# A decoder trunk kernel: small matrix products of the RWKV-7 recurrence on four array quarters, weight splits in pieces, operands built at other points

## The reference, cut to what matters

```python
def rwkv7_time_mix(p, mu, ...):            # 8 heads of 64
    r, k, v, zw, za, zg = _split(p + (prev - p) * mu, ...)
    kk = (k * k_k).reshape(B, T, H, N)
    kk = kk / jnp.maximum(jnp.sqrt(jnp.sum(kk * kk, -1, keepdims=True)), 1e-12)
    ...
    def step(S, inp):
        r_t, w_t, k_t, v_t, a_t, b_t = inp          # a = -kk, b = kk * a
        sa = jnp.einsum('bhij,bhj->bhi', S, a_t)
        S = S * w_t[:, :, None, :] + sa[..., None] * b_t[:, :, None, :] + v_t[..., None] * k_t[:, :, None, :]
        y = jnp.einsum('bhij,bhj->bhi', S, r_t)
        return S, y
    _, y = lax.scan(step, S0, xs)
    y = (y - mean) * lax.rsqrt(var + RWKV_LN_EPS)   # then ln_w, ln_b, bonus, gate
```

## Time and profile before

| | us |
|---|---|
| median of 3 runs | 1079.82 |
| lowest, highest | 1078.2, 1080.12 |
| the profiled execution | 1081.36 |
| its span (first to last instruction) | 1079.6 |
| of it PE busy | 1045.2 |
| DVE, POOL, ACT busy | 527.5, 496.8, 355.8 |

### The profile page before, as it was taken

One profiled execution on the slowest core, in us unless ns is written; L12 is line 12 of the kernel. 1 busy time (PEld: TensorE's weight loads), 2 busy tenths in 40 slices (PEclk: granted clock), 3 DMA queues, 4 the chain that ended last, 5 costly groups with the idle time before them and its releaser, 6 DMA issues.

```text
span 1079.6 us, 18610 instructions
## 1 busy us (share of the span) xinstructions
PE 1045.2 (97%) x7560; PEld 836.0 (77%) x7560; DVE 527.5 (49%) x882; ACT 355.8 (33%) x688; POOL 496.8 (46%) x409
## 2 busy tenths in 40 slices
PE   7989999999999999999989999999999999999997
PEld 6777778887787677766777777888888888888886
DVE  4775687466555545554552664144454545430004
ACT  4133332221322225444550445352222222221221
POOL 3365453113121446655777447534444444444462
PEclk9999999999999999999999999999999999999999
DMA  9334533002223453212112545603333333333322
GB/s 253 95 98 138 115 88 80 3 4 59 61 61 100 120 142 118 59 32 79 40 39 79 175 118 167 213 27 91 97 97 97 97 97 97 116 98 98 98 79 78
DMA packets 148784, 102.67 MB, mean 95 GB/s; under 512 B 20917, under 2 KB 131775, under 8 KB 148712
## 3 DMA queue, kind: packets, MB, share of 16 engines
q1 hardware_dynamic: 145516, 97.67, 31.9%
q10 hardware_dynamic: 3164, 3.97, 1.5%
q0 software_dynamic: 32, 0.00, 0.0%
HBM read 93.99 MB, written 7.63 MB: 94 GB/s over the span
## 4 chain that ended last, share of the span: by engine, by line
PE 83%; DVE 9%; POOL 4%; issue 2%; ACT 1%; DMA 1%; SPq 0%; ACTq 0%; DVEq 0%; POOLq 0%
PE ps L1546 17%; PE ps L1548 15%; PE ps L1547 15%; PE ps L1685 4%; PE ps L2001 4%; PE ps L2000 4%; PE ps L1999 4%; PE ps L1592 4%; PE ps L1845 3%; PE ps L1897 2%; DVE XF L1074 1%; PE ps L1921 1%; PE ps L1922 1%; PE ps L1923 1%; POOL WLO L605 1%
## 5 line engine op out<-in xcount | busy, mean ns | idle before, releaser
L605 POOL TENSOR_TENSOR WLO<-WRAW,WHI 128x1024 fp32r<-128x1024 f32 (+1 forms) x131 | 293.9, 2244 | 283.6 <-ACT WHI L723 158.0
L1546 PE MATMUL ps<-HHI,WHI 128*128 128x512 f32 x776 | 316.9, 408 | 5.1 <-POOL WLO L640 2.3
L1548 PE MATMUL ps<-HHI,WLO 128*128 128x512 f32 x776 | 304.3, 392 | 0.0
L1547 PE MATMUL ps<-HLO,WHI 128*128 128x512 f32 x776 | 304.1, 392 | 0.0
L1546 PEld LDWEIGHTS ps<-HHI,WHI 128*128 128x128 f32 x776 | 146.6, 189 | 57.7 <-issue 22.0
L1548 PEld LDWEIGHTS ps<-HHI,WLO 128*128 128x128 f32 x776 | 146.5, 189 | 32.0
L1547 PEld LDWEIGHTS ps<-HLO,WHI 128*128 128x128 f32 x776 | 146.8, 189 | 29.3 <-issue 1.9
L609 POOL CAST WHI<-WRAW 128x256 fp32r<-128x256 f32 (+1 forms) x78 | 49.2, 631 | 179.8 <-PE ps L1548 179.8
L723 ACT ACTIVATE WHI<-WRAW 128x1024 fp32r<-128x1024 f32 (+1 forms) x69 | 62.5, 907 | 159.4 <-PE ps L1548 82.0
L1504 DVE TENSOR_TENSOR FT<-FT 128x512 f32<-128x512 f32 x22 | 51.6, 2348 | 89.0 <-ACT FT L977 89.0
L870 ACT ACTIVATE EB<-EB,STAT 128x257 f32<-128x257 f32 (+5 forms) x96 | 50.4, 527 | 55.7 <-DVE STAT L1388 54.6
(11 more groups left out here) (311 smaller groups left out, 1608.1 us busy)
## 6 DMA issues: line engine op xcount, KB each, us to landing
WRAW<-in_w_in SPq DMA_DIRECT2D x47, 512.0 KB, 4.3
WRAW<-in_w_gate SPq DMA_DIRECT2D x22, 512.0 KB, 3.9
WRAW<-in_w_up SPq DMA_DIRECT2D x22, 512.0 KB, 3.9
WRAW<-in_w_down SPq DMA_DIRECT2D x22, 512.0 KB, 3.9
spilled<-SQ SPq DMA_DIRECT2D x21, 256.0 KB, 2.5
WRAW<-in_w_in SPq DMA_DIRECT2D x16, 256.0 KB, 3.6
WRAW<-in_w_branch SPq DMA_DIRECT2D x32, 128.0 KB, 2.9
WRAW<-in_w_out SPq DMA_DIRECT2D x8, 512.0 KB, 4.0
```

The lines of the kernel that those rows point to most:

```text
L605: return pool.tensor_tensor(lo[:, 0:chunks, :], WRAW[:, n % NRAW, 0:chunks, :], hi[:, 0:chunks, :].bitcast(F32), ALU.subtract)
L1546: pe.matmul(dst, WHI[:, s, k, :], hi, start=start, stop=False)
L1547: pe.matmul(dst, WHI[:, s, k, :], lo, start=False, stop=False)
L1548: return pe.matmul(dst, WLO[:, s, k, :], hi, start=False, stop=stop)
```

## The change

1. **Quarters.** XS, UI and T1 live in the other half of the partitions. U is formed `across` (operands in one half, result in the other: quadrants (0,1) and (1,0) in turns). In levels 1 to 4 the XC and XS products of a chunk are issued head by head: two of XC across, two of XS along the diagonal, into different PSUM banks. T1 and the state's part of y are interleaved likewise. ACT now copies XC of both chunks, then XS of both.
2. **Level 0.** PE forms both AM'·I and I·AM (64 matmuls per pass instead of 32) behind one increment; DVE makes XC and XS each in one op of 512 columns from PSUM.
3. **DVE's order.** evacs(pt + 1) and (pt + 2) move from ahead of level 1 into level 4; evacs(pt + 12) moves behind AR of the next pass; `scaled_bk(cp + 1)` moves from the first chunk to the end of the pass.
4. **Pieces.** Splitting by two chunks begins at job 28 (PIECE0) instead of 49.
5. **Operands.** XF of the second compression is built one quarter at a time (after NSA tile 5 and after mixed 4, 5, 6); its low and high part, the broadcast of kk and the product with it each come one RWKV tile later.
6. **Norm.** gn_bonus(1) comes ahead of inverse_split(1) on DVE.

```diff
-POOL_HI = [1] + list(range(NS0 + 4, MERGE0))
+PIECE0 = NS0 + 4
+POOL_HI = [1] + list(range(PIECE0, MERGE0))
...
-            for n in range(ATT_JOB):
+            for n in range(PIECE0):
                 whole_tile(n)
...
+            split_upto(int(_ends[ATT_JOB - NS0 - 1]))
             pool.wait_ge(gn_ok, 4)
...
-                if n == AT["rwkv", 7, 0]:
+                if n == AT["rwkv", 8, 0]:
                     x_high(1)
...
                 for lv in range(1, 6):
+                    if lv < 5:
+                        for c in range(2):
+                            act.wait_ge(xc_mm, 8 * cp + 2 * (lv - 1) + c + 1)
+                            act.activation(XC[:, 4 * c:4 * c + 4, :], R[c][:, 256:512].rearrange("p (a b) -> p a b", a=4),
+                                           ACT.Copy).then_inc(xc_ok, 1)
                     for c in range(2):
-                        slots = slice(4 * c, 4 * c + 4)
-                        if lv < 5:
-                            act.wait_ge(xc_mm, 8 * cp + 2 * (lv - 1) + c + 1)
-                            act.activation(XC[:, slots, :], R[c][:, 256:512].rearrange("p (a b) -> p a b", a=4),
-                                           ACT.Copy).then_inc(xc_ok, 1)
                         act.wait_ge(xs_mm, 10 * cp + 2 * (lv - 1) + c + 1)
...
-                    compress_in(i - 4)
+                    for quarter in range(4 if i == 4 else 1):
+                        compress_in(i - 4, quarter)
                     continue
                 mixed(n, i)
+                if 4 <= i < 7:
+                    compress_in(1, i - 3)
...
-                if i == 7:
+                if i == 8:
                     compress_low(1)
...
-                if i == 11:
+                if i == 12:
                     dve.wait_ge(kk_bc, 1)
...
+                if cp:
+                    evacs(PT_CP[cp - 1] + 12)
                 evacs(pt)
...
-                dve.tensor_tensor(XS[:, :, :], AM[:, 0, :, :], every("eye"), ALU.add).then_inc(x0_ok, 1)
-                for c in range(2):
-                    dve.wait_ge(u_mm, 12 * cp + c + 1)
-                    dve.tensor_tensor(XC[:, 4 * c:4 * c + 4, :], blocks(R[c][:, 0:256]), eyes, ALU.add).then_inc(xc0_ok, 1)
+                dve.wait_ge(u_mm, 11 * cp + 1)
+                dve.tensor_tensor(XC[:, :, :], blocks(R[0][:, :]), every("eye"), ALU.add).then_inc(xc0_ok, 1)
+                dve.tensor_tensor(XS[:, :, :], blocks(R[1][:, :]), every("eye"), ALU.add).then_inc(x0_ok, 1)
                 masked(0, 0)
                 masked(0, 1)
-                evacs(pt + 1)
-                evacs(pt + 2)
...
+                    if lv == 4:
+                        evacs(pt + 1)
+                        evacs(pt + 2)
...
             dve.wait_ge(norm_std, 3)
+            gn_bonus(1)
             inverse_split(1).then_inc(gn_rinv, 1)
-            gn_bonus(1)
...
-            upto(AT["rwkv", 11, 0] + 1)
+            upto(AT["rwkv", 12, 0] + 1)
             pe.wait_ge(kk_rinv, 1)
...
                 for c in range(2):
-                    pairs(R[c][:, 0:256], c, AM[:, 0, :, :], lambda p, j: mask("eye", C)[p, :]).then_inc(u_mm, 1)
+                    for m in range(4):
+                        j, cols = 4 * c + m, slice((4 * c + m) * C, (4 * c + m + 1) * C)
+                        for q in range(2):
+                            pe.matmul(R[0][half[q], cols], AM[half[q], 0, j, :], mask("eye", C)[half[q], :], start=True, stop=True)
+                            last = pe.matmul(R[1][half[1 - q], cols], mask("eye", C)[half[q], :], AM[half[q], 0, j, :],
+                                             start=True, stop=True)
+                last.then_inc(u_mm, 1)
...
-                        if lv < 5:
-                            pairs(R[c][:, 256:512], c, XS, lambda p, j: UI[p, j, :]).then_inc(xc_mm, 1)
-                        pairs(R[2 + c][:, 0:256], c, UI, lambda p, j: XS[p, j, :]).then_inc(xs_mm, 1)
+                        if lv == 5:
+                            pairs(R[2 + c][:, 0:256], c, UI, lambda p, j: XS[p, j, :]).then_inc(xs_mm, 1)
+                            continue
+                        for m in range(4):
+                            j, cols = 4 * c + m, slice(m * C, (m + 1) * C)
+                            for q in range(2):
+                                last_xc = pe.matmul(R[c][half[1 - q], 256 + m * C:256 + (m + 1) * C], XS[half[q], j, :],
+                                                    UI[half[q], j, :], start=True, stop=True)
+                            for p in half:
+                                last_xs = pe.matmul(R[2 + c][p, cols], UI[p, j, :], XS[p, j, :], start=True, stop=True)
```

More of the change, by code:

```diff
@@ L635, in split_upto @@
                         hi.then_inc(hi_piece, 1)
-                        pool.wait_ge(hi_piece, split["pieces"] - (n - ATT_JOB))
+                        pool.wait_ge(hi_piece, split["pieces"] - (n - PIECE0))
                     else:
@@ L1063, in gelu_end, with compress_in @@
                 dve.tensor_scalar(HG[:, :, :], HG[:, :, :], 0.5, None, ALU.mult).then_inc(hg_ok, 1)
[L1065 removed]
+            def compress_in(kv, quarter):
                 dve.wait_ge(dense_evac, group_of(AT["nsa", 4 + kv, 0]) + 1)
                 pe = PARC[:, PAR["pe"] + 32 * kv:PAR["pe"] + 32 * kv + 32].rearrange("p (j l) -> p j l", l=2)
[L1069 to L1075 removed]
+                l, g = quarter // 2, quarter % 2
+                p = slice(64 * g, 64 * g + 64)
+                src = NQ[p, 4 + kv, :]
+                v = bass.AP(src.tensor, src.offset + l, [list(src.ap[0]), [2, 16], [16, NCMP]])
+                dve.tensor_tensor(XF[kv][64 * l:64 * l + 64, :, g * NCMP:(g + 1) * NCMP], v,
+                                  pe[p, :, l:l + 1].broadcast_to([64, 16, NCMP]), ALU.add).then_inc(xf_ok, 1)
             def compress_low(kv):
@@ L1284, in _ @@
                                     R[2][0:64, 0:256].rearrange("p (m i) -> p m i", m=4)).then_inc(sa_dve, 1)
-                    if c == 0 and cp < 3:
-                        scaled_bk(cp + 1)
                     evacs(pt + 9 + 2 * c)
@@ L1290, in _ @@
                                       R[2][:, 0:256].rearrange("p (a b) -> p a b", a=4), ALU.add).then_inc(st_ok, 1)
-                evacs(pt + 12)
+                if cp < 3:
+                    scaled_bk(cp + 1)
+            evacs(PT_CP[3] + 12)
             for m in range(4):
@@ L1686, in pairs, with across @@
                     return last
+                def across(dst, c, lhsT, rhs):
+                    for m in range(4):
+                        for q in range(2):
+                            last = pe.matmul(dst[half[1 - q], m * C:(m + 1) * C], lhsT[half[q], 4 * c + m, :],
+                                             rhs[half[q], 4 * c + m, :], start=True, stop=True)
+                    return last
                 pe.wait_ge(am_ok, 6 * cp + 1)
@@ L1703, in _ @@
                         if lv == 1:
-                            pe.wait_ge(x0_ok, cp + 1)
                             pe.wait_ge(g_ok, 4 * cp + 2)
@@ L1721, in _ @@
                             h = 2 * m + q
-                            last = pe.matmul(R[c][half[q], m * C:(m + 1) * C], G[64:128, c, 4 * q + m, 0:C],
+                            last = pe.matmul(R[c][half[1 - q], m * C:(m + 1) * C], G[64:128, c, 4 * q + m, 0:C],
                                              SV[64:128, c, h * HD:(h + 1) * HD], start=m == 0, stop=False,
@@ L1732, in _ @@
                     for m in range(4):
-                        for p in half:
-                            last = pe.matmul(R[c][p, m * C:(m + 1) * C], AR[p, m, c, 0:C], ST[p, g % 2, m, :],
-                                             start=False, stop=True, skip_group_check=True)
-                    last.then_inc(t1_mm, 1)
-                    for m in range(4):
-                        for p in half:
-                            pe.matmul(R[4 + c][p, m * C:(m + 1) * C], ST[p, g % 2, m, :], AR[p, m, c, C:P],
+                        cols = slice(m * C, (m + 1) * C)
+                        for q in range(2):
+                            last = pe.matmul(R[c][half[1 - q], cols], AR[half[q], m, c, 0:C], ST[half[q], g % 2, m, :],
+                                             start=False, stop=True, skip_group_check=True)
+                        if m == 3:
+                            last.then_inc(t1_mm, 1)
+                        for p in half:
+                            pe.matmul(R[4 + c][p, cols], ST[p, g % 2, m, :], AR[p, m, c, C:P],
                                       start=m == 0, stop=False, skip_group_check=True)
@@ L1745, in _ @@
                         for q in range(2):
-                            last = pe.matmul(R[2 + q][0:64, m * C:(m + 1) * C], XS[half[q], 4 * c + m, :], T1[half[q], c, m, :],
+                            last = pe.matmul(R[2 + q][0:64, m * C:(m + 1) * C], XS[half[1 - q], 4 * c + m, :], T1[half[1 - q], c, m, :],
```

23 lines of the change are left out of this document (9 added, 14 removed).

## The result

| | before | changed |
|---|---|---|
| median, us | 1079.12 (4 runs) | 1060.24 (4 runs) |
| lowest, highest | 1078.2, 1080.12 | 1057.63, 1061.71 |
| span of the profiled execution | 1079.6 | 1057.9 |

The ratio of the runs is 0.9819 (95% interval 0.9807 to 0.9832). The medians lie 18.9 us apart: the changed kernel is inside the range of 1047 to 1068, and 5.6 us slower than the 1054.6 that was forecast. The two profiled executions differ by more, 21.6 us (1081.36 and 1059.73). That of before took longer than any of its timed runs (the slowest of all rounds was 1080.87).

What follows compares the result with a forecast made beforehand. PE, busy 1045.2 of 1079.6 us, was taken as the bound. Terms 11.2 + 3.8 + 4.1 + 3.9 + 3.2 + 1.0 - 2.0 = 25.2 us off the median 1079.82 gave 1054.6, range 1047 to 1068.

Steps and rivals of the forecast that it cites:

- Full rate on four quadrants: PE's small recurrence products: 32 matmuls on four quadrants start in 0.48 us, 14.5 ns each instead of 29.
- B: Rival on PE's quadrants: starts limited to 24 ns, 32 matmuls take 0.78 us, levels bound by PE; 1065.5 us, chance 0.12.
- C: Rival on PE's quadrants: those of the same rows do not overlap, rate stays one per 29 ns; 1073.4 us, chance 0.08.
- Levels, 11.2: Recurrence levels 1 to 4: period falls from 3.07 to 2.34 us, 2.8 us per pass, 11.2 us in four passes.
- T1 and y, 3.8: T1 and state products in the recurrence: the pair takes one group's time, 0.48 us less in 8 chunks, 3.8 us.
- Waits of the recurrence, 4.1: PE's waits for UI, ST and AR: DVE's new order leaves 0.6 of 4.7 us, winning 4.1 us.
- XF 3.9, HINV 3.2: Input phase: PE's waits for PSH (2.2 us) and HINV (1.5) go, with the half clock behind each; 3.9 and 3.2 us.
- Norm, 1.0: Norm behind the recurrence: gn_bonus(1) no longer stands behind an inverse, so PE's wait for AA goes; 1.0 us.
- Pieces, -2.0: POOL's splitting by two chunks from the fifth spilled job: costs 2.0 us, bounds +1 and -4; a small gain not excluded.
- A: The forecast's own case: full rate on all four quadrants, 1054.6 us, own bounds 1048 to 1060, chance 0.66.
- rival E: Pieces cost more than 4 us, POOL the bound ahead of the norm: 1057 to 1062, chance 0.05; or below 1047, 0.04.
- Rival D: Recurrence levels: the new gap in each brings half clock, 34 us over 20 levels; slower, 1088.6 us, chance 0.05.

Runs made afterwards that it cites:

- e11: The kernel before with everything of the change except the quarters (halves, products and level 0 as before): 1070.69 us, ratio 0.9918.
- e9: The kernel before with the quarters alone (halves, order of products, level 0 as changed), all else as before: 1069.26 us, ratio 0.9905.
- e10: The changed kernel with whole tiles split up to the attention and DVE's old order in the recurrence: 1061.98 us, ratio 0.9839.
- e5: The changed kernel with DVE's order of the recurrence as before: 1059.58 us, ratio 0.9817.
- e1: The changed kernel with whole tiles instead of pieces up to the attention (jobs 28 to 48): 1058.59 us, ratio 0.9812.
- e4: The changed kernel with the input phase as before (XF in a row, its low part, kk broadcast and product one tile earlier): 1065.52 us, ratio 0.9881.

## Why the prediction was right

The sign, the mechanism and the range held; the size was 25.2 forecast, 21.6 in the profiled pair and 18.9 in the medians. Term by term, against the traces:

- **Full rate on four quadrants**: right. 14.7 ns per start in level 0. Rivals B and C fall. The floor of about 25 ns which the Trainium skill states ("TensorE: Matmul & The Clock Gate", "Wait — 56ns, not 53.3ns?") is not seen: on different quadrants starts lie mostly 6 or 7 ns apart, with a step of 38 behind each four, 14.7 ns in the mean. The rule of the same page of the Trainium skill that weight loads overlap only across row groups (Part 3) would have kept 29 ns; all quadrants of both row groups ran at once.
- **What the trace of before already said against C**, and the prediction did not read. That only the two quadrants of the diagonal are used is not true of L1722: both of its operands lie in the lower rows for every head, and its results in both halves of the columns. So it uses two quadrants of the same row half:

```profile
195.36 1.09 PE L1722 MATMUL ps<-SV,G 64*64 64x64 f32 x29
```

29 matmuls start within 0.87 us, 30 ns each, where a single quadrant at 58 ns would need 1.7 us. That quadrants of the same rows do not overlap, C's first half, could have been ruled out from this row.
- **Levels, 11.2**: mis-sized, 9.1. The chain's sum of 2.32 us was 0.14 too short, 0.10 in the hand-over from ACT to U and 0.04 in U itself (0.02 of it was allowed for). But the last of the four levels, with the transposes, won 0.8 (3.39 for 4.19) where I had counted 0.6, so that an undisturbed pass gave 2.7 of my 2.8. What cost 1.7 in the first two passes is 0.3 of "DVE must fit ... does" (it fits alone, and not beside POOL) and mostly a term that the sum put at nothing: pauses of PE that no wait explains. The slower levels of before and of e11 have none over 0.15 us; with quarters they show in every trace but at other places, up to 1.0 us in the last pass of e9 and e10. Their cause stays open.
- **T1 and y, 3.8**: 3.5. **Level 0, nothing**: right.
- **Waits of the recurrence, 4.1**: 5.5 (e11), but not for the reason that the text gave alone. With the quarters in place, undoing DVE's order brings back 1.1 us of waits for ST (e5), undoing the pieces 1.1 us in the level with the stretched AM (e1), and undoing both 6.1 us of time (e10). What each would win without the quarters no run shows. I had priced the pieces' share as "a small gain cannot be excluded".
- **XF 3.9, HINV 3.2**: 3.8 and 3.3 in the profiled pair; 5.3 instead of 7.1 in the medians (e4). Half clock behind these waits is not in every execution, which fits that difference and is not shown to be all of it.
- **Norm, 1.0**: 1.6. Whole tiles would have taken it back (e1 +0.5, with a wait of 1.4 us for AA), a second unforeseen gain of the pieces.
- **Pieces, -2.0**: 2.2 ahead of the passes, right in size and place. The end of the code was missed: POOL's zero fill of VCZ stands behind the last piece on the same queue, and its 1.1 us more of waiting, with the half clock that followed, cost 2.7. Together that is 4.9, more than the bound of 4 that this term had. The step left out was what else POOL does behind the last tile: I went through the tiles only.

How near a thing the range was has to be said as well. The measured 1060.24 lies 0.2 us outside A's own bounds (1048 to 1060); it is inside the range because that took in rival B, which fell. And it lies in the 1057 to 1062 of rival E, whose condition, pieces that cost more than 4 us, came true, though through the zero fill behind the norm and not, as E said, ahead of it.

The sum again with what was measured: 9.1 + 3.5 + 5.5 + 3.8 + 3.3 + 1.6 - 2.2 - 2.7 - 0.4 (first tile) = 21.5, the 21.6 of the two profiled executions. The other 2.7 us down to the 18.9 of the medians are a matter of which executions were profiled: that of before was the slowest seen of its kernel. Half clock has a part in it (three of the four runs of the changed kernel have a mean clock of 0.994 to 0.996, the fastest, 1057.63, has 0.998), but not all: the runs of e1 lie between 1056.92 and 1061.15 with 0.998 each. The rest of that spread stays open.

Rival D (new gaps bring half clock into the recurrence) fell: 1.00 throughout, with 154.50 of 158.30 us busy.

## What to carry to other kernels

Small products on different quadrants of the array run side by side, even when issued kind after kind; it is enough to place operands and results so that neighbours use other quadrants, and turns by hand pay only where the group itself is on the path. When a group gets shorter than the loop around it, price the loop by start-to-start times of waits that did bind, and call a hand-over that no row shows an estimate. Before one trace's stage sum is put down to an edit, compare two traces that have the same code in that stage. And work that is cut into short pieces costs where its queue is nearly full and pays where another engine works beside it: look for both, and for what stands behind the last piece.
